# A fused S5, attention and mixture-of-experts layer: a reordered front and shared-expert steps moved into the first expert batch

## The reference, cut to what matters

```
hn = rms_norm(h);  u, q, k, v = split(hn @ w_in)
y_ssm = s5(u)                       # complex diagonal state space, gelu, glu
y_att = stick_breaking(rms_norm(q), rms_norm(k), v)
h = h + concat(rms_norm(y_ssm), rms_norm(y_att)) @ w_out
t = rms_norm(h)
gate = top-8 of 64 experts, from the 4 best of 8 groups
h = h + sum_e gate_e * ((silu(t@w1_e) * (t@w3_e)) @ w2_e)
      + (silu(t@s1) * (t@s3)) @ s2  # the shared expert
```

## Time and profile before

| | us |
|---|---|
| median of 3 runs | 614.69 (614.52 to 615.71) |
| the profiled execution | 615.7 |
| its span, first to last instruction | 614.0 |
| PE busy | 584.4 (95%) |
| DVE / ACT / POOL busy | 244.1 / 144.3 / 17.5 |
| moved by DMA | 224.98 MB |

### The profile page before, as it was taken

How to read it: one execution, slowest core, us unless ns; L and a number is a source line. 1 busy time by engine, 2 the same in 40 slices (tenths; PEclk the granted TensorE clock), 3 DMA queues, 4 the chain that set the end, 5 groups by cost and what they waited for, 6 DMA issues and landing times.

```text
span 614.0 us, 9983 instructions
## 1 busy us (share of the span) xinstructions
PE 584.4 (95%) x3970; PEld 267.2 (44%) x3970; DVE 244.1 (40%) x652; ACT 144.3 (23%) x306; POOL 17.5 (3%) x65
## 2 busy tenths in 40 slices
PE   8999699999999998899889999999999999999786
PEld 6455455646553434334333434343443434343322
DVE  3999672557841334123232331322232313223122
ACT  6644464213421111102111202020211212120101
POOL 3001021000000000000000000000000000000000
PEclk9999899999999999999999999999999999999998
DMA  8972536995499999999999999999999999999994
GB/s 317 428 290 99 67 121 247 425 389 199 132 359 425 432 419 404 425 429 422 427 423 426 426 425 423 426 423 428 422 425 423 429 420 431 420 431 424 422 404 154
DMA packets 30110, 224.98 MB, mean 366 GB/s; under 512 B 6752, under 2 KB 7264, under 8 KB 12896
## 3 DMA queue, kind: packets, MB, share of 16 engines
q1 hardware_dynamic: 29344, 223.17, 89.1%
q10 hardware_dynamic: 720, 1.18, 0.6%
HBM read 222.11 MB, written 1.05 MB: 363 GB/s over the span
## 4 chain that ended last, share of the span: by engine, by line
PE 73%; DMA 12%; DVE 11%; ACT 1%; issue 1%; SPq 1%; DVEq 0%; ACTq 0%
PE bank L728 70%; DMA ring<-in_e_w 6%; DMA wreg<-in_e_w 4%; DVE ring L1501 4%; DVE reg_c L1501 2%; DMA ring<-in_bc 2%; PE bank L1125 1%; PE bank L823 1%; DVE small L1501 1%; DVE wreg L1501 1%; PE bank L1152 0%; DVE small L1640 0%; DVE reg_ab L1501 0%; DVE ring L1507 0%; SPq L325 0%
## 5 line engine op out<-in xcount | busy, mean ns | idle before, releaser
L728 PE MATMUL bank<-ring,wreg 128*32 128x512 f32 (+2 forms) x1272 | 251.4, 598 | 2.8 <-DMA wreg<-in_e_w 2.3
L728 PE MATMUL bank<-wreg 128*32 128x512 f32 (+5 forms) x445 | 146.8, 591 | 0.8 <-DMA ring<-in_e_w 0.7
L728 PEld LDWEIGHTS bank<-ring,wreg 128*32 128x32 f32 (+1 forms) x1272 | 71.8, 120 | 110.8 <-issue 108.2
L1501 DVE TENSOR_TENSOR wreg<-wreg,bank 128x256 f32<-128x256 f32 x28 | 11.8, 422 | 166.7 <-ACT wreg L1428 166.7
L728 PE MATMUL bank<-wreg,reg_ab 128*128 128x512 f32 (+1 forms) x192 | 75.6, 544 | 0.0
L728 PE MATMUL bank<-reg_ab,wreg 128*64 128x512 f32 (+2 forms) x192 | 70.8, 559 | 0.9 <-DVE reg_ab L1744 0.9
L728 PE MATMUL bank<-reg_d 128*128 128x512 f32 (+1 forms) x140 | 63.5, 592 | 2.9 <-DVE reg_d L1945 2.9
L728 PE MATMUL bank<-side,wreg 128*32 128x512 f32 (+2 forms) x150 | 60.7, 603 | 3.3 <-DMA ring<-in_e_w 3.3
L1260 ACT ACTIVATE reg_d<-bank 128x512 f32<-128x512 f32 (+2 forms) x47 | 22.2, 473 | 164.1 <-PE bank L728 100.4
L1501 DVE TENSOR_TENSOR acc<-acc,bank 128x512 f32<-128x512 f32 (+1 forms) x70 | 47.1, 673 | 30.5 <-PE bank L728 29.4
L728 PEld LDWEIGHTS bank<-wreg 128*32 128x32 f32 (+4 forms) x445 | 39.5, 123 | 37.8 <-issue 36.7
(11 more groups left out here) (198 smaller groups left out, 388.8 us busy)
## 6 DMA issues: line engine op xcount, KB each, us to landing
ring<-in_e_w SPq DMA_DIRECT2D x36, 2048.0 KB, 21.4
ring<-in_e_w SPq DMA_DIRECT2D x46, 1024.0 KB, 20.4
wreg<-in_e_w SPq DMA_DIRECT2D x14, 2048.0 KB, 22.1
reg_ab<-in_e_w SPq DMA_DIRECT2D x8, 2048.0 KB, 21.7
wreg<-in_e_w SPq DMA_DIRECT2D x12, 1024.0 KB, 15.8
side<-in_e_w SPq DMA_DIRECT2D x9, 1024.0 KB, 18.1
wreg<-in_w_in SPq DMA_DIRECT2D x2, 2048.0 KB, 24.8
wreg<-in_w_out SPq DMA_DIRECT2D x1, 4096.0 KB, 12.7
```

The costliest lines, as they stand in the source:

```text
L728: return nc.tensor.matmul(out_, lhsT, rhs, start=start, stop=stop, **kw)
L1501: return nc.vector.tensor_tensor(out_, a, b, op)
```

## The change

It has a front of its own and a new order around batch 0:

- SP issues `bc_in` behind two of the four blocks of `w_in`, not behind all four.
- The three `cmul` for the turn of one chunk go: the angle is multiplied by 8 before sine and cosine are taken, on 32 columns in the place of 16 (`th2`).
- `token_scales` leaves DVE; ACT does it by logarithm and exponential with one correcting step, behind the table load, which is moved there from ahead of the first exponential.
- `sums_of_heads` and `norm_qk` become `norm_heads(0)` and `norm_heads(1)`, each with a chain of its own on 16 columns; PE waits for `qk_normed` 4.
- `turn_y` stands inside `project_attention(0)`.
- The roots of h use fused steps (`start_root`, `half_step`, `full_step`); DVE's copies of the turned h stand between them; `hs` is scaled by ACT (`scale_h`).
- DVE's choice of groups has two operations fewer; `P0` is made without the two copies of `place`.
- PE does 9 shared steps ahead of the first gather and 7 in batch 0 (`shared_rest`), in banks 2 and 3. The gather does not wait for `pgT_evac`. ACT takes all four results of the gather.
- Batch 0 (`first_batch`): behind `up(0, 1)` come `turn(0, 0)`, the 7 shared steps, `turn(0, 1)`, two gathers, the turn of the shared expert, both `down`, and only then the other two gathers.
- SP's two loads behind `sh_part` 2 and `sh_up` 2 move behind that of `up_done` 2; `rest` takes the place of `hs`, so room 5's last piece waits for `parts_ready`, and stands behind that of `up_part`.

```diff
@@ sync
             for n in range(KT // 2):
                 ks = slice(2 * n, 2 * n + 2)
+                if n == 2:
+                    sp.dma_start(bc_in, I["bc"]).then_inc(S["bc_in"], 16)
                 sp.dma_start(w_in[:, 0, ks], wi[0, :, ks]).then_inc(wu_in[n], 16)
-            sp.dma_start(bc_in, I["bc"]).then_inc(S["bc_in"], 16)
...
-            sp.wait_ge(S["sh_part"], 2)
-            sp.dma_start(room13[4][:, 2048:3072], w13v[EB + 1, :, 2048:3072]).then_inc(S["pair_in"], 16)
-            sp.wait_ge(S["sh_up"], 2)
-            sp.dma_start(room13[4][:, 3072:4096], w13v[EB + 1, :, 3072:4096]).then_inc(w13_in[4], 16)
-            sp.wait_ge(S["rest_ready"], 1)
-            sp.wait_ge(S["gath_done"], 4)
-            sp.dma_start(room13[5][:, 2048:4096], w13v[EB + 2, :, 2048:4096]).then_inc(w13_in[5], 16)
             sp.wait_ge(S["up_part"], 1)
             sp.dma_start(room13[0][:, 0:2048], w13v[EB + 3, :, 0:2048]).then_inc(S["part_in"], 16)
+            sp.wait_ge(S["gath_done"], 4)
+            sp.wait_ge(S["parts_ready"], 1)
+            sp.dma_start(room13[5][:, 2048:4096], w13v[EB + 2, :, 2048:4096]).then_inc(w13_in[5], 16)
             sp.wait_ge(S["up_done"], 1)
...
             sp.wait_ge(S["up_done"], 2)
             load13(2, e1)
+            sp.wait_ge(S["sh_part"], 2)
+            sp.dma_start(room13[4][:, 2048:3072], w13v[EB + 1, :, 2048:3072]).then_inc(S["pair_in"], 16)
+            sp.wait_ge(S["sh_up"], 2)
+            sp.dma_start(room13[4][:, 3072:4096], w13v[EB + 1, :, 3072:4096]).then_inc(w13_in[4], 16)
             e2 = expert(SMALL_AT + 2)
             load13(3, e2)
@@ tensor
-            shared_up(0, range(0, 2))
+            shared_up(0, range(0, 1))
             router_logits(1)
-            shared_up(1, range(0, 2))
-            shared_up(0, range(2, 4))
-            shared_up(1, range(2, 4))
-            shared_up(0, range(4, 6))
+            shared_up(1, range(0, 1))
+            for k in range(1, 4):
+                shared_up(0, range(k, k + 1))
+                shared_up(1, range(k, k + 1))
...
-            shared_up(1, range(4, 6))
-            shared_up(0, range(6, 7))
+            shared_up(0, range(4, 5))
...
+            def first_batch():
+                pe.wait_ge(S["pgT_evac"], 1)
+                pe.wait_ge(S["xa"], 2)
+                pe.wait_ge(S["xd"], 2)
+                up(0, 0, None, "plain")
+                list_items()
+                turn_slots(0, "plain")
+                up(0, 1, None, "plain")
+                turn(0, 0)
+                shared_rest()
+                turn(0, 1)
...
+                gather_slices(0)
+                gather_slices(1)
+                shared_turn()
+                pe.wait_ge(S["sh_actT"], 2)
+                pe.wait_ge(S["route_ready"], 1)
+                down(0, 0, None, "plain")
+                down(0, 1, None, "plain")
+                pe.wait_ge(S["xa"], 3)
+                gather_slices(2)
+                pe.wait_ge(S["xd"], 3)
+                gather_slices(3)
@@ scalar
+            nc.scalar.preload_act_table_set("natural_log_exp_and_others")
+            act.wait_ge(S["ssx_ready"], 4)
+            nc.scalar.activation(tok_nh, ssx, ACT.Identity, bias=neg_half_eps, scale=-0.5 / D)
+            nc.scalar.activation(tok_ln, ssx, ACT.Ln, bias=eps_col, scale=1.0 / D).then_inc(S["act_chain"], 1)
...
-            nc.scalar.preload_act_table_set("natural_log_exp_and_others")
             exp_log(0)
@@ vector
-            dve.wait_ge(S["U_ready"], 1)
-            cur, nxt = [cosv, sinv], [t1, t2]
-            tq = [t3, t4, e8r, e8i]
-            for _ in range(3):
-                cmul(nxt, cur, cur, tq)
-                cur, nxt = nxt, cur
...
-            step(ts(gmask, rk1, float(TOPG), ALU.is_lt))
-            step(ts(rk1, gmask, -1.0, ALU.add, BIG, ALU.mult))
+            step(ts(lim, rk1, TOPG - 0.5, ALU.subtract, -LIMIT, ALU.mult))
-            step(tt(s4, b4, gmask.unsqueeze(3).to_broadcast([128, 2, NG, GE]), ALU.mult))
-            step(tt(s4, s4, rk1.unsqueeze(3).to_broadcast([128, 2, NG, GE]), ALU.add))
+            step(tt(s4, b4, lim.unsqueeze(3).to_broadcast([128, 2, NG, GE]), ALU.min))
```

More of the change, by code:

```diff
@@ L133, in build @@
         lam_re, li, ls = (first_in[:, GAINS + PR * i:GAINS + PR * i + PR] for i in range(3))
-        lr, mag, th, cosv, sinv, lbr, lbi, t1, t2, t3, t4, cor, coi, den, e8r, e8i, rho = (
-            par(PR) for _ in range(17))
+        lr, mag, lbr, lbi, t1, t2, t3, t4, cor, coi, den, rho = (par(PR) for _ in range(12))
+        th2, cos2, sin2, turns = (par(2 * PR) for _ in range(4))
+        th, cosv, sinv = (w[:, 0:PR] for w in (th2, cos2, sin2))
+        chunk_turn = [w[:, PR:2 * PR] for w in (cos2, sin2)]
         PW = [par(9 * PR).rearrange("p (k r) -> p k r", k=9) for _ in range(2)]
@@ L184, in build @@
                  for i in range(3)]
-        rest = reg_d[:, 0:2048].rearrange("p (a k m) -> p a k m", a=2, k=KT)
+        rest = hs
+        silu_s = [reg_d[:, F * a:F * a + F] for a in range(2)]
+        act_s = [reg_d[:, F * (2 + a):F * (2 + a) + F] for a in range(2)]
         Pm = rx(EB * SLOTS).bitcast(BF16).rearrange("p (a e s) -> p a e s", a=2, e=EB)
@@ L255, in build @@
         ssqk = sm(32)
+        eps_col, neg_half_eps, three_halves = sm(1), sm(1), sm(1)
+        tok_ln, tok_y, tok_nh, tok_t = (par(4) for _ in range(4))
         rsx, rs_nat = rsx4[:, 0:2], rsx4[:, 2:4]
@@ L923, in project_attention, with turn_y @@
                     if a == 0 and hf == 0:
+                        turn_y()
                         sums_of_squares(sqa, 2, 1)
-            project_attention(0)
[L928 to L932, removed]
-                last.then_inc(S["yT_done"], 1)
+            def turn_y():
+                pe.wait_ge(S["y5_gelu"], 2)
+                for a in range(2):
+                    for q in range(4):
+                        j = 2 * q + a
+                        last = nc.tensor.transpose(ps[a][:, 128 * q:128 * q + 128], ygel[:, 128 * j:128 * j + 128], ident[:, :])
+                    last.then_inc(S["yT_done"], 1)
+            project_attention(0)
             pe.wait_ge(S["glu_in"], 16)
@@ L1207, in batch @@
                     up(it, 0, before, kind, loads)
-                    if before is None:
-                        list_items()
-                    else:
-                        combine(before, was, shared)
+                    combine(before, was, shared)
                     turn_slots(it, kind)
@@ L1473, in batch @@
                     y_out(it, 1)
-            batch(0)
+            silu(0, 0)
+            slots_out(0)
+            silu(0, 1)
+            turned(0, 0)
+            shared_silu(0)
+            shared_silu(1)
+            turned(0, 1)
+            gathered(1, 0)
+            for a in range(2):
+                act.wait_ge(S["sh_T"], a + 1)
+                copy(actT_s[a], ps[2 + a][:, 0:256].rearrange("p (j s) -> p j s", j=2)).then_inc(S["sh_actT"], 1)
+            y_out(0, 0)
+            y_out(0, 1)
+            gathered(1, 1)
             act.wait_ge(S["route_ready"], 1)
@@ L1851, in _ @@
             dve.wait_ge(S["slots_ready"], 1)
-            place(0, 0)
+            for a in range(2):
+                last = tt(P0[:, a], iota.unsqueeze(1).to_broadcast([128, EB, SLOTS]),
+                          pos[:, a, 0:EB].unsqueeze(2).to_broadcast([128, EB, SLOTS]), ALU.is_equal)
+            last.then_inc(S["P_ready"], 1)
             c = slice(0, E)
@@ L1991, in _ @@
                         *(N_FIXED + PLAIN_AT + EB * s for s in range(N_FIRST - FIRST_PLAIN + 1)))
-            batch(None, at=first_at[1])
+            activate(0, 0)
+            take_list()
+            slots_out(0)
+            place(1, first_at[1])
+            place_gates(1)
+            activate(0, 1)
+            shared_activate(0)
+            shared_activate(1)
+            gathered(1, 0)
+            y_out(0, 0)
+            y_out(0, 1)
+            gathered(1, 1)
             x_before = dve.value_load(n_before[0:1, :], min_val=N_NORMAL - 2, max_val=N_NORMAL - 2 + MAX_FULL)
```

212 lines of the change are left out of this document (126 added, 86 removed).

## The result

| | before | changed |
|---|---|---|
| median | 614.88 (614.52 to 615.71, 4 runs) | 610.54 (610.03 to 611.55, 4 runs) |
| the profiled execution | 615.7 | 611.55 |
| its span | 614.0 | 609.6 |
| PE / DVE / ACT busy | 584.4 / 244.1 / 144.3 | 583.2 / 237.5 / 152.5 |

The ratio is 0.993 (95% interval 0.9912 to 0.9947), 4.3 us less. Forecast were 609.4 and a range of 605.6 to 612.2.

The account below looks back on a forecast made before the run. The weight stream, gated by TensorE's release of rooms, plus a fixed tail was taken as the bound. Batch 1 starting 4.5 us sooner plus 0.8 from the DMA engines gave -5.3, 609.4 us, range 605.6 to 612.2.

Parts of the forecast that it names:

- What bounds the kernel: Whole kernel: the weight stream plus a fixed tail sets the end, which moves as much as TensorE's event at 237.81.
- the event at 237.81: `down_done` 6, for which SyncE was held at the stream's last hole; forecast to come 4.5 us sooner, near 233.3.
- Front: From the start to the first exponential: turns of q and k 4.95 us sooner, exponential at 68.5 instead of 75.45.
- From there to batch 0: First exponential to batch 0: `turn_y` saves 0.95 us, slots and gathers 4.5; batch 0 starts 12.4 sooner, near 151.0.
- Batch 0 gets the work back: Inside batch 0: seven shared steps, a turn, its copies and the last evacuation add 8.2 us, so batch 1 gains 4.5.
- SyncE: Load queue: `route_ready` loads near 162, `down_done` 2 loads near 182.7, room 4's two pieces at 176 to 178, cost 0.
- the 0.8 us for the engines that had never run dry: Hole at 238 to 240 us: busy DMA engines now lose less, a gain of 0.8 us (0 to 4).
- Rival 1: DMA: the slowest engine sets the pace and moves with the burst of `down_done` 2; -8.3 us, 606.4, chance 0.18.
- Rival 2: Before the first exponential: VectorE's gain is smaller; +0.7 us in the extreme, about -2.5 halfway, 612.2; chance 0.19.
- Rival 3: Batch 0's seven steps cost more than the start gains, 5.45 against 8.2 us; 2.7 later, 617.4; chance 0.05.
- the turning point: The gain before the first exponential at which the change becomes neither faster nor slower: 2.75 us.
- Rival 4: Behind 240 us: TensorE, 96% busy, becomes the bound and the early start is lost; within 0.2%, chance 0.03.

Follow-up runs that it names:

- e10: The changed kernel with `bc_in` issued behind all four blocks of `w_in` again: 615.91 us, ratio 1.001 to the kernel before.
- e7: The changed kernel with the seven shared steps ahead of the first gather again, SyncE's new order kept: 612.71 us, ratio 0.9958 to the kernel before.
- e5: The changed kernel run again unaltered, on another chip: 610.11 us, ratio 0.9914 to the kernel before.
- e6: The changed kernel with batch 0's last two gathers ahead of both down-projections again: 610.32 us, ratio 0.9919 to the kernel before.
- e3: The changed kernel with 28 idle matmuls (6.5 us) ahead of batch 8's first product: 613.12 us, ratio 0.9965 to the kernel before.
- e9: The changed kernel with 30 idle matmuls (6.86 us) ahead of the turns of q and k: 617.01 us, ratio 1.003 to the kernel before.
- e1: The changed kernel with four of batch 0's seven shared steps left out, so the layer is incomplete: 606.78 us, ratio 0.985 to the kernel before.
- e2: The changed kernel with 28 idle matmuls (6.5 us) ahead of batch 1's first product: 616.23 us, ratio 1.0013 to the kernel before.
- e4: The changed kernel with 28 idle matmuls (6.5 us) ahead of the last plain batch, near 520 us: 609.74 us, ratio 0.9904 to the kernel before.
- e11: The changed kernel with two of batch 0's seven shared steps moved into earlier TensorE waits: 609.08 us, ratio 0.9909 to the kernel before.
- e8: The changed kernel with 9 and 7 idle matmuls in the two longest waits for the last weights: 609.26 us, ratio 0.9899 to the kernel before.
- e12: The changed kernel with the moved steps of e11 and the idle matmuls of e8 together: 607.71 us, ratio 0.9884 to the kernel before.

## Why the prediction was right

**What bounds the kernel.** Right as far as the stream goes: it followed the event at 237.81 one to one, in eleven kernels, on both sides of the kernel before. For the time it is right to some 2 us.

**Front.** `bc_in` -2.69 (forecast -2.8), q and k at 63.45 (63.8), turns at 63.80 (63.95) in 1.91 us (2.0), first exponential 68.12 (68.5). Of the 7.33 us at the exponential 5.12 are the earlier start of the turns and 1.62 the clock: 3.53 became 1.91 since no idle time stood ahead. e10 shows that the clock's part is a step, not a slope: behind 3.25 us of idle time the turns took 3.68, behind the 5.01 of the kernel before 3.53, and behind none 1.91; so 3.4 us on VectorE cost 6.0 on TensorE. The exponential now waits 0.62 us for the clamp and for no table load. No drain shows behind the moved load either: it lies from 25.90 to 27.18, and the next activation starts at 27.19.

**From there to batch 0.** The glu products -7.96 against -7.33 at the exponential, so `turn_y` brought 0.63 (0.95). Batch 0 at 151.16 (151.0). Its wait ahead did not go, as I had booked with 0.3, but grew from 0.31 to 0.86.

**Batch 0 gets the work back.** +8.07 for +8.2, in the parts named: 6.17 the steps, 0.70 the turn, 0.50 its copies, 1.02 the last evacuation (8.39, of which 0.3 overlap). Batch 1 at 186.12 (185.8), the event at 233.62 (233.3).

**SyncE.** The two pieces went out at 170.57 and 174.01, sooner than the 176 to 178 forecast, and cost nothing. The loads behind `route_ready` went out at 162.45 (162), those behind `down_done` 2 at 183.72 (182.7). I had not seen what e7 shows, that the old place of the steps with the new place of the pieces would have cost 3.7 us.

**The term that was too large** is the 0.8 us for the engines that had never run dry. TensorE's event gave 4.19; the stream gained 4.6, so 0.4 of the 0.8 can be seen there, and the last landing gained 4.24, so none of it arrived. By 184 us the changed kernel was 10.2 us of stream ahead. It lost 1.8 of this by 190, 2.6 more by 230 (378 to 392 GB/s between 200 and 230 us, 415 to 434 before) and the rest by 250. Two windows of the kernel before, beside those of the changed one above:

```profile
184.00:190.00 6.00, 6.00 (x60) 1.69 (x52) 0.99 (x2) 0.60 (x1) 0.00 (x0) 1.00 1.03 434
230.00:234.00 4.00, 3.32 (x54) 3.03 (x55) 1.03 (x3) 1.66 (x6) 0.00 (x0) 1.00 1.05 436
```

Being early does not help where the rooms are not free.

**Where luck helped.** The forecast was -5.3. The first comparison gave -4.3 and e5 gave -5.5, which looks like a hit, but in both the event moved 4.2 to 4.3 us and the stream 4.6 to 4.7. What e5 has more lies, as far as its one profile shows, in its tail, which the sum had left alone, and in the spread of the runs.

**The rivals.** Rival 1 (the slowest engine, -8.3) did not happen. The burst of `down_done` 2 went out 6.7 us sooner and the stream gained 4.6; in e6 that burst went out 0.8 us later than in the changed kernel and the stream stayed as it was. The stream left the event by more than 0.6 us only in e3, whose delay stands behind it. Rival 2 (the front gives less) did not happen, but e10 is its case: with `bc_in` back batch 1 starts at 192.13, 1.8 us later than before where the rival's extreme had 0.7, and no gain is left. Rival 3 (slower) had the right mechanism: e9 took back 8.2 us, its event came 4.0 later than before and it was 1.9 us slower, where the rival said 2.7 for both at 6.95 taken back. By the event the turning point lies, as said, where some 3 us of the front's gain are left; by the time, drawn straight between the changed kernel and e9, where 1 to 2 are. Rival 4 fell with e1 and e2.

**The tail.** I took the 9.33 us behind the last landing for fixed. They were the same in the first profile after the change, so the sum did not suffer. But they are not fixed: e5, the same kernel, went through this work in 8.43 us with a wait of 0.59 in it, e4 in 7.92. So the 9.2 contain some 1.3 us of low clock. In the one profiled execution of each, the clock behind the last wait is 0.66 to 0.71 in the kernel before, the changed kernel, e2, e6 and e10, and 1.00 in e1, e3, e4, e5, e7, e9 and e11. That may be part of why most times lie below what the stream gives.

## What to carry to other kernels

Where a stream of loads is gated by the engine that uses them up, follow that engine's first release behind the last hole. In these kernels the stream moved by what this event moved, to within 0.6 us, work added or taken away ahead of it counted in full, and the stream's own lead ahead of it counted for almost nothing. An idle stretch ahead of a dependent stage costs more than its length where the clock falls in it, so a small load placed ahead of a large one in a queue can be worth twice the wait that it removes (here 6.0 us of TensorE for 2.5 of VectorE's wait). And before a tail is taken for fixed, its clock should be read. And where a step that frees a buffer is moved, the load into that buffer has to be moved in the issuing queue with it.

## What the runs showed that I had not expected

- The granted clock fell behind short waits: 2.10 and 1.59 us near the end gave 0.66 in the 5 us read behind each, while 1.28 us at the same place left 1.00 in e5, and a wait of 1.34 us gave 0.70 in e9, while 1.35 us at the same place left 1.00 in the changed kernel.
- Sixteen idle products in the last two long waits kept it at 1.00 in all eight runs of e8 and e12 (0.999 to 1.0 in the mean). The median was 0.85 us lower with them in e8 and 1.4 in e12, neither clear of the spread.
- 6.5 us of additional work for TensorE cost 5 to 6 us ahead of batch 1, about half ahead of batch 8 and nothing near 520 us: TensorE's share of 96% said nothing of where it could be late.
